# A hybrid decoder step on one core: a new order of the rounding and splitting work around a Strassen-form feed-forward, and of the weight sums made ahead of it

## The reference

```python
h = rms_norm(x); z = h @ w_in
o_att = sliding-window attention with sinks      # 8 query heads, 2 kv heads
o_ml  = mLSTM, chunkwise, with output norm and gate
x = x + concat(o_att, o_ml) @ w_out
h2 = rms_norm(x)
g, u = split(h2 @ w_ffn_in)                      # 1024 x 5632
x = x + (silu(causal_dwconv3(g)) * u) @ w_down   # 2816 x 1024
```

## Time and profile before

| | |
|---|---|
| median of 3 runs | 2353.27 us (2352.03 to 2362.79) |
| profiled execution | 2354.42 us |
| its span in the trace | 2352.7 us, mean granted TensorE clock 0.990 |
| TensorE matmul, weight load | 2242.8 us (95%), 1977.7 us (84%) |
| VectorE | 1470.7 us (63%) |
| ScalarE | 892.7 us (38%) |
| GpSimd | 907.6 us (39%) |
| HBM traffic | 310.39 MB read, 126.07 MB written |

### The profile page before, as it was taken

One profiled execution on the slowest core, in us unless ns is written; L12 is line 12 of the kernel. 1 busy time (PEld: TensorE's weight loads), 2 busy tenths in 40 slices (PEclk: granted clock), 3 DMA queues, 4 the chain that ended last, 5 costly groups with the idle time before them and its releaser, 6 DMA issues.

```text
span 2352.7 us, 34529 instructions
## 1 busy us (share of the span) xinstructions
PE 2242.8 (95%) x13423; PEld 1977.7 (84%) x13423; DVE 1470.7 (63%) x2139; ACT 892.7 (38%) x1524; POOL 907.6 (39%) x855
## 2 busy tenths in 40 slices
PE   7999999999999999989979999989999999999999
PEld 6889878877777888888879999989999988888887
DVE  5566656765664456777786666786666664445543
ACT  4555622222232324444454333453433433233331
POOL 4333316877320424333342333342333330245730
PEclk9999999999999999999999999999999999999999
DMA  8433227999354555666674555564555545686454
GB/s 277 159 127 116 85 86 231 306 283 284 117 169 169 173 196 195 217 198 202 199 254 148 176 160 172 166 228 147 170 162 170 170 148 197 216 285 201 144 174 165
DMA packets 253837, 437.79 MB, mean 186 GB/s; under 512 B 29419, under 2 KB 171911, under 8 KB 251607
## 3 DMA queue, kind: packets, MB, share of 16 engines
q1 hardware_dynamic: 253643, 435.52, 56.1%
q0 software_dynamic: 32, 0.07, 0.0%
HBM read 310.39 MB, written 126.07 MB: 186 GB/s over the span
## 4 chain that ended last, share of the span: by engine, by line
PE 44%; DVE 6%; ACT 2%; issue 1%; DMA 1%; POOL 0%; SPq 0%; ACTq 0%; DVEq 0%
PE bank L2923 9%; PE bank L2924 9%; PE bank L2925 9%; PE bank L114 6%; PE bank L116 6%; PE bank L115 6%; DVE late_b_lo L3245 3%; DVE late_t_lo L3245 1%; DVE late_up L3272 1%; ACT late_a_hi L3039 1%; DVE late_gp L3272 1%; ACT late_gp L3076 0%; DMA late_a_raw<-h_parts 0%; ACT late_b_hi L3050 0%; DVE late_t L3284 0%
## 5 line engine op out<-in xcount | busy, mean ns | idle before, releaser
L3470 POOL TENSOR_TENSOR late_t<-late_t,late_up 128x768 f32<-128x768 f32 (+1 forms) x66 | 143.4, 2172 | 562.7 <-DVE late_up L3272 562.7
L2923 PE MATMUL bank<-late_a_hi,late_b_hi 128*128 128x384 f32 (+1 forms) x1056 | 345.4, 327 | 7.3 <-DVE late_gp L3272 2.0
L2924 PE MATMUL bank<-late_a_lo,late_b_hi 128*128 128x384 f32 (+1 forms) x1056 | 343.7, 325 | 0.0
L2925 PE MATMUL bank<-late_a_hi,late_b_lo 128*128 128x384 f32 (+1 forms) x1056 | 342.4, 324 | 0.0
L2923 PE MATMUL bank<-late_a_hi,late_t_hi 128*128 128x384 f32 (+1 forms) x792 | 264.5, 334 | 58.7 <-DVE late_t_lo L3245 29.1
L3245 DVE TENSOR_TENSOR late_b_lo<-late_c_raw,late_b_hi 128x1024 fp32r<-128x1024 f32 x128 | 260.5, 2035 | 7.2 <-ACT late_b_hi L3050 7.2
L2924 PE MATMUL bank<-late_a_lo,late_t_hi 128*128 128x384 f32 (+1 forms) x792 | 258.6, 327 | 0.0
L2925 PE MATMUL bank<-late_a_hi,late_t_lo 128*128 128x384 f32 (+1 forms) x792 | 258.1, 326 | 0.0
L114 PE MATMUL bank<-late_e_hi,late_y_a_hi 128*128 128x512 f32 x616 | 241.7, 392 | 2.7 <-DVE late_e_lo L3302 2.1
L116 PE MATMUL bank<-late_e_hi,late_y_a_lo 128*128 128x512 f32 x616 | 241.9, 393 | 0.0
L115 PE MATMUL bank<-late_e_lo,late_y_a_hi 128*128 128x512 f32 x616 | 241.0, 391 | 0.0
(11 more groups left out here) (388 smaller groups left out, 4977.3 us busy)
## 6 DMA issues: line engine op xcount, KB each, us to landing
late_t_raw<-weight_sums SPq DMA_DIRECT2D x66, 768.0 KB, 7.0
...
```

The costliest lines, as they stand in the source:

```text
L2923: nc.tensor.matmul(out, w_h, hi[:, c, :], start=first, stop=False, skip_group_check=True)
L2924: nc.tensor.matmul(out, w_h, lo[:, c, :], start=False, stop=False, skip_group_check=True)
L2925: ins_ = nc.tensor.matmul(out, w_l, hi[:, c, :], start=False, stop=last, skip_group_check=True)
L3470: nc.gpsimd.tensor_tensor(t_of(r)[:, x, 0:G.TG], t_of(r)[:, x, 0:G.TG], up[:, x, 0:G.TG], ALU.mult).then_inc(act_made, 1)
```

## The change

1. Weight sums: tiles 0 to 12 instead of 2 to 12; four items in tiles 0 to 4, three in tiles 5 to 12. T2 and T4 are stored together, so an item has three stores instead of four. `store_os` moves behind tile 13.
2. Pieces of `t`: piece 2 holds T2 and T4 (1024 columns), piece 3 T3 (512).
3. TensorE: `sample_down` moves between the units.
4. SP: `load_d` moves ahead of `load_b(0, ...)`.
5. ScalarE and VectorE: a new order in `step`.

```diff
     if t.c + 2 < NT:
         load_m(t.c + 2)
     for pair in range(2):
-        if SUM_FROM < t.c <= SUM_TO:
-            ahead.store(sp, t.c - 1, 2 * pair)
-            ahead.store(sp, t.c - 1, 2 * pair + 1)
-        if SUM_FROM <= t.c < SUM_TO:
-            ahead.load(sp, ins, t.c, 2 * pair)
-            ahead.load(sp, ins, t.c, 2 * pair + 1)
+        if 0 < t.c <= SUM_TO:
+            for n in ahead.pair(t.c - 1, pair):
+                ahead.store(sp, t.c - 1, n)
+        if t.c < SUM_TO:
+            for n in ahead.pair(t.c, pair):
+                ahead.load(sp, ins, t.c, n)
     if 1 <= t.c <= samp.c:
         store_o(sp, t - 1)
     if is_sample(t - 1):
...
     load_m(1)
     period(once)
     load_states()
+    tiles_each(period, 1, SUM_TO + 1)
     store_os(sp, o_dram, start)
-    tiles_each(period, 1, NT)
+    tiles_each(period, SUM_TO + 1, NT)
     sp.wait_ge(start.os_out, 16 * 32)
     load_out_start()

...
 A11, S2, A12, S3, S1, A22, S4 = range(7)
 B11, B21, B22, T1, T2, T3, T4 = range(7)
 PRODUCTS = ((A11, B11, 0), (S2, T2, 1), (A12, B21, 0), (S3, T3, 1), (S1, T1, 2), (A22, T4, 1), (S4, B22, 2))
-PIECE_OF = (0, 2, 0, 3, 1, 3, 1)
+PIECE_OF = (0, 2, 0, 3, 1, 2, 1)
 A_ORDER = (A11, S2, A12, S3, S1, A22, S4)
 A_SUMS = ((S1, S3, A22, ALU.add), (S2, S1, A11, ALU.subtract), (S3, A11, S3, ALU.subtract), (S4, A12, S2, ALU.subtract))

...


 PIECES = 4
-SUM_FROM = 2
-SUM_ITEMS = 4 * NP
-SUM_TO = SUM_FROM + SUM_ITEMS // PIECES
+SUM_ITEMS = (4, 4, 4, 4, 4, 3, 3, 3, 3, 3, 3, 3, 3)
+SUM_TO = len(SUM_ITEMS)
+assert sum(SUM_ITEMS) == 4 * NP
 IMAGE = KH * 2 * P


...
     sp.wait_ge(self.made, self.count(slot, n, 3))
     dst = self.dram[unit]
     sp.dma_start(dst[:, 2 * e * 2 * P:2 * (e + 1) * 2 * P], self.top[n].rearrange("p c x n -> p (c x n)")).then_inc(self.moved[n], 16)
-    t = dst[:, IMAGE:IMAGE + 3 * KH * P].rearrange("p (a c n) -> p a c n", a=3, c=KH)[:, :, 2 * e:2 * e + 2, :]
-    sp.dma_start(t[:, 0], self.diff[n]).then_inc(self.moved[n], 16)
-    for x in range(2):
-        sp.dma_start(t[:, 1 + x], self.low[n][:, :, x, :]).then_inc(self.moved[n], 16)
+    at_ = IMAGE + 2 * e * P
+    sp.dma_start(dst[:, at_:at_ + 2 * P].rearrange("p (c n) -> p c n", c=2), self.diff[n]).then_inc(self.moved[n], 16)
+    at_ = IMAGE + KH * P + 2 * e * 2 * P
+    sp.dma_start(dst[:, at_:at_ + 4 * P], self.low[n].rearrange("p c x n -> p (c x n)")).then_inc(self.moved[n], 16)

 def wait_all(self, eng):
     for n in range(PIECES):
-        eng.wait_ge(self.moved[n], self.moves(SUM_TO))
+        eng.wait_ge(self.moved[n], self.moves(SUM_TO, n))


 def half_tile(h, j):
...
         x = q
         cut = lambda a: a[:, :].rearrange("p (c n) -> p c n", c=KC)[:, :, x * P:(x + 1) * P]
         return cut(raw), cut(lo), hi[:, x, :].rearrange("p (c n) -> p c n", c=KC)
-    n = slice(2 * KH * P, 3 * KH * P) if q == 2 else slice(0, 2 * KH * P)
+    n = slice(KH * P, 3 * KH * P) if q == 2 else slice(0, KH * P)
     return t_raw[u][:, n], t_lo[u][:, n], t_hi[u][:, :, :].rearrange("p a n -> p (a n)")[:, n]

 def b_parts(u, b, c):

     if b in (T2, T3, T4):
-        at_ = ((T3, T4, T2).index(b) * KH + c) * P
+        at_ = {T3: c, T4: KH + 2 * c, T2: KH + 2 * c + 1}[b] * P
         n = slice(at_, at_ + P)
         return t_hi[u][:, :, :].rearrange("p a n -> p (a n)")[:, n], t_lo[u][:, n]
     x, part = {B11: (0, 0), B21: (0, 1), T1: (1, 0), B22: (1, 1)}[b]
...
     r = (G, i)
     if r != FIRST:
         load_t(1, r)
-        load_b(0, after(r))
         if before(r) != FIRST and before(r)[0].sample:
             load_d(before(r))
+        load_b(0, after(r))
         if r == LAST:
             load_turn(0)
         store_act(before(r))
...
     for i in range(NP):
         r = (G, i)
         unit(r, 0)
+        p = before(r)
+        if p is not None and p[0].sample:
+            sample_down(p)
         if G.index == 1 and i == 0:
             turn_conv_s()
             pe.wait_ge(rows_kept, 2)
         unit(r, 1)
-        p = before(r)
-        if p is not None and p[0].sample:
-            sample_down(p)
 turn_conv_p()
 for n in range(NDOWN):
     down_turn(n)
...
     late_a = i == NP - 1 and nxt is not None
     if turned:
         round_a(G, 4)
-    if p is not None:
+        keep_first(r, 0, 0)
+        round_a(G, 5)
+        keep_first(r, 0, 1)
+        round_a(G, 6)
         round_b(r, 1, 0)
-    keep_first(r, 0, 0)
-    if turned:
-        round_a(G, 5)
-    if p is not None:
         round_b(r, 1, 1)
-    keep_first(r, 0, 1)
-    if turned:
-        round_a(G, 6)
-    if p is None:
+    elif p is None:
+        keep_first(r, 0, 0)
+        keep_first(r, 0, 1)
         keep_h(final)
         x_normed.wait(act, final)
         round_b(r, 1, 0)
         round_b(r, 1, 1)
+    else:
+        round_b(r, 1, 0)
+        keep_first(r, 0, 0)
+        round_b(r, 1, 1)
+        keep_first(r, 0, 1)
     round_b(r, 1, 2)
     round_b(r, 1, 3)
     if p is not None and p[0].sample:
         round_d(p, 0)
         round_acts(p)
+        round_d(p, 1)
     if G.index == 1 and i == 0:
         keep_conv_s()
     conv_head(r, 0)
...
     keep_first(r, 1, 0)
     round_b(nxt, 0, 0)
     silu_of(r, 0)
-    if p is not None and p[0].sample:
-        round_d(p, 1)
-    keep_first(r, 1, 1)
     if late_a:
+        keep_first(r, 1, 1)
         round_a(nxt[0], 0)
-    silu_of(r, 1)
+        round_b(nxt, 0, 1)
+        round_b(nxt, 0, 2)
+        round_a(nxt[0], 1)
+        silu_of(r, 1)
+        round_a(nxt[0], 2)
+        round_b(nxt, 0, 3)
+        round_a(nxt[0], 3)
+    else:
+        round_b(nxt, 0, 1)
+        round_b(nxt, 0, 2)
+        keep_first(r, 1, 1)
+        round_b(nxt, 0, 3)
+        silu_of(r, 1)
     if nxt is None:
         for n in range(RINGS):
             round_turn(n)
-    round_b(nxt, 0, 1)
-    round_b(nxt, 0, 2)
-    if late_a:
-        round_a(nxt[0], 1)
-        round_a(nxt[0], 2)
-    round_b(nxt, 0, 3)
-    if late_a:
-        round_a(nxt[0], 3)

 for p in positions:
     if p.c >= 1 and p is not final:
...
     turned = i == 0 and p is not None
     late_a = i == NP - 1 and nxt is not None
     if turned:
+        combine(r, 0, 0)
         split_a(G, 4)
-    if p is not None:
+        split_a(G, 5)
+        combine(r, 0, 1)
+        split_a(G, 6)
+        combine(r, 0, 2)
         split_b(r, 1, 0)
-    combine(r, 0, 0)
-    if turned:
-        split_a(G, 5)
-    if p is not None:
+        combine(r, 0, 3)
         split_b(r, 1, 1)
-    combine(r, 0, 1)
-    if turned:
-        split_a(G, 6)
-    if p is None:
+        split_b(r, 1, 2)
+        combine(r, 0, 4)
+        split_b(r, 1, 3)
+    elif p is None:
+        combine(r, 0, 0)
+        combine(r, 0, 1)
         split_b(r, 1, 0)
+        combine(r, 0, 2)
         split_b(r, 1, 1)
-    split_b(r, 1, 2)
-    combine(r, 0, 2)
-    split_b(r, 1, 3)
-    combine(r, 0, 3)
+        combine(r, 0, 3)
+        split_b(r, 1, 2)
+        combine(r, 0, 4)
+        split_b(r, 1, 3)
+    else:
+        split_b(r, 1, 0)
+        combine(r, 0, 0)
+        split_b(r, 1, 1)
+        combine(r, 0, 1)
+        split_b(r, 1, 2)
+        combine(r, 0, 2)
+        split_b(r, 1, 3)
+        combine(r, 0, 3)
+        if p[0].sample:
+            split_acts(p)
+        combine(r, 0, 4)
+    if turned and p[0].sample:
+        split_acts(p)
     if p is not None and p[0].sample:
         split_d(p, 0)
-        split_acts(p)
-    combine(r, 0, 4)
+        split_d(p, 1)
+    tap(r, 0, 1)
+    tap(r, 0, 2)
     if G.sample:
         combine(r, 1, 0)
-        tap(r, 0, 1)
+        tap(r, 1, 1)
+        split_b(nxt, 0, 0)
         combine(r, 1, 1)
-        tap(r, 0, 2)
+        tap(r, 1, 2)
         combine(r, 1, 2)
-        if p is not None:
-            split_d(p, 1)
+        if late_a:
+            split_a(nxt[0], 0)
+        split_b(nxt, 0, 1)
+        combine(r, 1, 3)
+        split_b(nxt, 0, 2)
+        if late_a:
+            split_a(nxt[0], 1)
+        combine(r, 1, 4)
+    elif late_a:
+        combine(r, 1, 0)
+        split_b(nxt, 0, 0)
+        split_a(nxt[0], 0)
+        combine(r, 1, 1)
+        split_b(nxt, 0, 1)
+        combine(r, 1, 2)
+        split_b(nxt, 0, 2)
+        split_a(nxt[0], 1)
+        combine(r, 1, 3)
         tap(r, 1, 1)
         tap(r, 1, 2)
+        combine(r, 1, 4)
     else:
-        tap(r, 0, 1)
+        tap(r, 1, 1)
         combine(r, 1, 0)
-        tap(r, 0, 2)
+        tap(r, 1, 2)
+        split_b(nxt, 0, 0)
+        split_b(nxt, 0, 1)
         combine(r, 1, 1)
-        if p[0].sample:
-            split_d(p, 1)
-        tap(r, 1, 1)
+        split_b(nxt, 0, 2)
         combine(r, 1, 2)
-        tap(r, 1, 2)
-    split_b(nxt, 0, 0)
+        split_b(nxt, 0, 3)
+        combine(r, 1, 3)
+        combine(r, 1, 4)
+    if G.sample and not late_a:
+        split_b(nxt, 0, 3)
     if late_a:
-        split_a(nxt[0], 0)
-    combine(r, 1, 3)
+        split_a(nxt[0], 2)
+        split_b(nxt, 0, 3)
+        split_a(nxt[0], 3)
     if nxt is None:
         split_turn(0)
```

(13 more changed lines are left out.)

18 lines of the change are left out of this document (9 added, 9 removed).

## The result

The changed kernel takes 2326.11 us (median of 4 runs, 2325.06 to 2332.53), the kernel before 2353.24 beside it: ratio 0.9882, 95% interval 0.985 to 0.9913. The profiled execution took 2326.44, its span is 2324.7 against 2352.7: 28.0 us less.

The account below looks back on a forecast made before the run. TensorE, busy 95% of the span, was taken to lose time waiting for VectorE's splits and combines. Terms -25.3 + 13 - 3.3 - 3.5 - 3.5 + 6.2 - 8.6 = -25.0 from 2353.3 gave 2328 us, range 2313 to 2344.

Parts of the forecast that it names:

- The main case: Whole kernel: all terms come as forecast, sum -25.0 us, time 2328 us; chance 0.44.
- sample rounds: Ten feed-forward rounds: down products between units stop TensorE 2.9 us, clock falls in two of three; +1.3 each, +13.
- first round: First feed-forward round: combine (0,2) waits behind one split instead of three, saving 1.7 and a 1.6 clock fall: -3.3.
- end: Last round and down projection: the forecast gave no term for them.
- prompt rounds: Prompt rounds: u0 splits moved ahead of combines remove the T2 and T3 waits, 1.33 us in each of 19: -25.3.
- first turn and its round: Turn to group 1: -3.5 for an earlier combine (0,0), +6.2 for 4.6 idle and a clock fall at the down products.
- second turn, without the prompt round ahead of it: Turn to group 2: combine (0,0) no longer behind the splits of A slot 4 and B: -3.5, bounds +3 and -8.
- mLSTM and all ahead of the feed-forward: mLSTM tiles: sums spread over thirteen tiles shorten GpSimd's tile to about 19 us, under TensorE's 20.25: -8.6.
- The late-landing rival: Prompt rounds: split 2's load lands later than 11 us and stalls u1; 2.0 us in 19 rounds, 2366; chance 0.06.
- The T3 wait stays in part: Sample rounds: a split meeting the first gate takes 2.49, combine (0,0) ends at 5.5, T3 waits 0.7 us a round.
- the 7 us that it would have taken off the sum: Sample rounds: by the skill's rule a split issued first leaves combine (0,0) on time, sum 7 us lower; not followed.
- the bound named for combine (1,1) behind the split of slot 0: Turns: combine (1,1) stands behind the split of A slot 0, whose load lands late; bound of +3.

Follow-up runs that it names:

- experiment 6: Changed kernel with VectorE's two splits for the prompt's first down product ahead of the last round's combine (1,4): 2324.24 us, ratio 0.9856.
- experiment 9: Changed kernel with VectorE's taps (1,1), (1,2) before the turn to group 2 right behind combine (1,0), and combine (1,1) ahead of slot 0's split: 2326.11 us.
- experiment 7: Changed kernel with group 0's very first round reordered on VectorE: combine (1,0), two taps, combine (1,1), two taps, combine (1,2): 2325.56 us, ratio 0.9866.
- experiment 8: Changed kernel with silu (1) behind the rounding of slots 2 and 3 at both turns, and combine (1,1) ahead of slot 0's split at the second: 2328.3 us.
- experiment 2: Changed kernel with the samples' down products put back behind unit 1 on TensorE alone: 2288.53 us, ratio 0.97 to the kernel before.
- the nine traces: Traces with the changed kernel's code ahead of the feed-forward, its own among them; the feed-forward begins between 886.88 and 891.25 us, median 888.52.
- experiment 10: Changed kernel with down products behind unit 1, first-round combine (1,0) between taps, second turn's taps early, end splits ahead of combine (1,3): 2275.46 us, ratio 0.9654.

## Why the prediction was right, and where it was not

2328 was forecast, 2326.1 came: -25.0 against -27.1 by the medians and -28.0 by the spans of the two profiled executions. The main case held, but three of its terms missed by 4 to 7 us each (sample rounds, first round, end) and made up for one another. That the sum came out so near is luck in that part.

| step | predicted | measured |
|---|---|---|
| prompt rounds | -25.3 (19 x 1.33) | -28.3 (19 x 1.49) |
| sample rounds | +13 | +5.6 |
| first round | -3.3 | +1.7 |
| first turn and its round | -3.5 + 6.2 | +1.4 |
| second turn, without the prompt round ahead of it | -3.5 | -2.4 |
| mLSTM and all ahead of the feed-forward | -8.6 | -10.4 |
| end | 0 | +4.4 |
| sum | -25.0 | -28.0 |

**Prompt rounds: right.** No wait before T2 or T3 in any of them, 29.49 for the 29.7 given. The two steps hide 1.49 and not 1.33, since the distance to an unbroken round is 30.98 - 29.49. All 19 lose both waits. One of them, the last of group 1, lies in the window of the second turn; its 1.5 us are counted here and not there. The late-landing rival shows nowhere; every steady round has TensorE full.

**Sample rounds: the mechanism right, one term mis-sized.** The stop is 2.82 us in each of the ten (2.9 forecast), released by the split of the down weights as named; the clock fell after seven of ten (two in three forecast), and a round with a fall is 29.9 against 28.4, so a fall costs 1.5, nearly the 1.6 of the earlier trace rows. In experiments 6 and 9 the same ten rounds have five falls and take 291.6 and 291.8 instead of 294.4. The step that failed is "The T3 wait stays in part", put at 0.7 a round: it is gone, and the 0.1 before T2 with it. A round is 29.44 and not 30.04, 6 of the 7.4 us between forecast and measurement. The rest is the base: the nine rounds of the earlier trace rows average 28.72, all ten 28.88. In the changed kernel split 2 started 0.26 us before the first gate and took its usual length, where I had it meet the gate and take 2.49:

```profile
1091.89 1.21 DVE L3255 TENSOR_TENSOR late_t_lo<-late_t_raw,late_t_hi 128x1024 fp32r<-128x1024 f32 x1
1092.15 4.10 POOL L3510 TENSOR_TENSOR late_t<-late_t,late_up 128x576 f32<-128x576 f32 x2 [16.55 <-DVE late_up L3282]
...
1094.88 2.46 DVE L3255 TENSOR_TENSOR late_b_lo<-late_c_raw,late_b_hi 128x1024 fp32r<-128x1024 f32 x1
1097.26 0.45 DVE L3282 TENSOR_TENSOR late_gp<-bank,late_gp 128x288 f32<-128x288 f32 x1
```

Combine (0,0) ends 4.8 us into the round (1097.71, the round starts at 1092.92), just when T3 is due; the prediction had it at 5.5. Here GpSimd paid: its two gates took 4.10 together. The Trainium skill, page "SBUF — State Buffer", section "Who interferes with whom", says that the order of issue decides which of the two waits; this trace agrees (1.21 for the one that came first, 2.46 for the split that came second), and the 7 us that it would have taken off the sum were nearly the right ones.

**First round: wrong.** "Behind one split it waits about 0.3" held (0.30). The step that failed is that the sum stopped there: combine (1,0) now stood behind four taps, these met GpSimd's four sums for the last sample rows, and product 3 of unit 1 waited 3.19 us, with a clock fall behind it. -3.3 + 3.2 + 1.6 = +1.5 is near the +1.7 measured. Experiment 7 shows the cause.

**Turns: right in sum.** Forecast for the first turn's stop was 4.6 and a fall; it is 4.3 and a fall. At the second, the bound named for combine (1,1) behind the split of slot 0 came true (2.3 us), and a wait of 4.0 for ScalarE that was not foreseen; -2.4 is what is left of the 13 that were to be had. Experiments 8 and 9 show where they came from: the first from the split of slot 0 ahead of combine (1,1), the second from the taps, whose place in the order held ScalarE. With both gone, other waits of 1.3 and 2.1 us come up behind the splits of the slots, and 3.4 us are gained in all.

**mLSTM: right, a little dear.** Thirteen tiles gave -7.1 where -8.6 stood, for one slip of 1.9 us in the tile behind the last with four items: that five tiles with four cost TensorE nothing because six did failed. Another 2.8 came in the stretch behind them (57.99 for 60.82). A wait of 1.0 for a copy of the sample state shows in the trace of before. Of the other 1.8, 1.7 are the clock's, which stood at half for 6.8 us in the changed kernel and for 10.2 in the kernel before (row of before):

```profile
594.83:655.65 60.82, 59.78 (x335) 43.91 (x336) 37.50 (x90) 15.11 (x35) 15.42 (x17) 0.92 0.24 83
```

They are not the change's: experiments 2 and 8, with the changed kernel's code there, take 59.54 and 59.55. Over the nine traces the feed-forward begins 8.7 us earlier than before in the median, so of the -10.4 some 1.7 belong to the one execution.

**The end: wrong.** It was costed at nothing. Both last gates now close together, and the last split of the first down product met one (2.29 for 0.68): 3.9 us of idling for 2.1 before, and 6.8 us at half clock behind it. Experiments 6 and 10 show it.

What the sum could not show is the larger thing. It priced the sample rounds at +13 against the kernel before and credited the move of the down products with the T2 wait that the new order takes away by itself. Against the new order without the move, the move costs 42.6 us (experiment 2).
